# Moving half of one branch's softmax scaling to VectorE, and reordering scores, transposes and scaling

## The reference, cut to what matters

```python
s = einsum('bqhgd,bkhd->bhgqk', q, k) * scale      # + mask, + sink in swa
p = softmax(s)
o = einsum('bhgqk,bkhd->bqhgd', p, v)
x = x + gate * (sum over branches of sigmoid(g) * ((o * silu(z)) @ w_o)) @ w_out
```

## Time and profile before

| | us |
|---|---|
| median of 3 runs (1754.3 to 1757.47) | 1756.91 |
| the profiled execution | 1756.88 |
| its span in the profile | 1755.1 |

### The profile page before, as it was taken

The page is one execution under the profiler, slowest core; times in us unless marked ns, Lnnn a source line. Parts: engine busy times, 40 slices in busy tenths (PEclk is TensorE's granted clock), DMA queues, the critical chain, the costliest instruction groups (busy, mean ns, idle before and its releaser), DMA issues.

```text
span 1755.1 us, 26992 instructions
## 1 busy us (share of the span) xinstructions
PE 1679.7 (96%) x10400; PEld 1471.6 (84%) x10400; DVE 1037.7 (59%) x2164; ACT 1049.0 (60%) x1919; POOL 625.0 (36%) x426
## 2 busy tenths in 40 slices
PE   7899999999999999999999999999999998999997
PEld 3778888889888899999889996788888887888787
DVE  6445766665566655545774556566676666555633
ACT  3435777776667767765221254678777678777322
POOL 2433333333333332323322344344344433333442
PEclk9999999999999999999999999999999999999999
DMA  9111111111121112012635222111122221212642
GB/s 332 40 37 29 26 46 37 49 31 49 49 55 49 42 31 55 26 48 57 219 117 197 90 87 61 41 38 46 51 53 67 72 73 32 69 52 53 204 148 93
DMA packets 178531, 129.51 MB, mean 74 GB/s; under 512 B 21658, under 2 KB 167652, under 8 KB 178404
## 3 DMA queue, kind: packets, MB, share of 16 engines
q1 hardware_dynamic: 174240, 115.36, 23.0%
q10 hardware_dynamic: 2884, 8.24, 1.3%
q0 software_dynamic: 1280, 4.20, 0.7%
HBM read 123.58 MB, written 4.19 MB: 73 GB/s over the span
## 4 chain that ended last, share of the span: by engine, by line
PE 77%; DVE 11%; ACT 8%; issue 3%; DMA 1%; POOL 1%; SPq 0%; DVEq 0%; ACTq 0%
PE acc L1393 56%; PE wide L1444 6%; PE ptp L1462 6%; PE pv L1475 4%; PE pv L1476 3%; DVE nmax L2051 2%; ACT e L1710 2%; DVE pt L2076 1%; ACT w_hi L1627 1%; DVE k_m L1579 1%; DVE q_s L1579 1%; ACT k_m L1570 1%; DVE k_s L1579 1%; DMA w_raw<-in_ada_w 1%; ACT e L1717 0%
## 5 line engine op out<-in xcount | busy, mean ns | idle before, releaser
L1834 POOL TENSOR_TENSOR w_lo<-w_raw,w_hi 128x1024 fp32r<-128x1024 f32 (+2 forms) x192 | 390.9, 2039 | 566.4 <-ACT w_hi L1627 565.0
L1393 PE MATMUL acc<-h_hi,w_hi 128*128 128x512 f32 (+2 forms) x1320 | 466.1, 354 | 13.0 <-DVE lf L1954 5.1
L1393 PE MATMUL acc<-h_hi,w_lo 128*128 128x512 f32 (+2 forms) x1320 | 462.4, 351 | 0.0
L1393 PE MATMUL acc<-h_lo,w_hi 128*128 128x512 f32 (+2 forms) x1320 | 458.6, 351 | 0.5 <-POOL h_lo L1896 0.5
L1393 PEld LDWEIGHTS acc<-h_hi,w_hi 128*128 128x128 f32 (+1 forms) x1320 | 249.5, 189 | 52.0 <-issue 12.4
L1725 ACT ACTIVATE pt<-ptp 128x512 fp32r<-128x512 f32 (+3 forms) x312 | 165.9, 563 | 198.2 <-PE ptp L1462 196.4
L1393 PEld LDWEIGHTS acc<-h_hi,w_lo 128*128 128x128 f32 (+1 forms) x1320 | 249.8, 189 | 34.0
L1393 PEld LDWEIGHTS acc<-h_lo,w_hi 128*128 128x128 f32 (+1 forms) x1320 | 246.9, 189 | 34.8 <-POOL h_lo L1896 0.9
L2051 DVE TENSOR_REDUCE nmax<-wide 128x1 f32<-128x768 f32 (+3 forms) x240 | 190.0, 792 | 112.1 <-PE wide L1444 108.6
L1888 POOL TENSOR_TENSOR o_t<-o_half,o_t 64x256 f32<-64x256 f32 x120 | 91.9, 766 | 436.9 <-DVE o_half L2083 434.8
L1717 ACT ACTIVATE e<-e,einv 128x768 f32<-128x768 f32 (+3 forms) x240 | 193.4, 806 | 57.2 <-DVE einv L2068 56.8
(11 more groups left out here) (215 smaller groups left out, 3065.8 us busy)
## 6 DMA issues: line engine op xcount, KB each, us to landing
w_raw<-in_w_in SPq DMA_DIRECT2D x102, 512.0 KB, 3.9
w_raw<-in_ada_w SPq DMA_DIRECT2D x48, 512.0 KB, 5.3
w_raw<-in_w_out SPq DMA_DIRECT2D x16, 512.0 KB, 3.5
w_raw<-in_w_in SPq DMA_DIRECT2D x16, 256.0 KB, 3.2
w_raw<-in_w_o_mla SPq DMA_DIRECT2D x16, 256.0 KB, 2.7
w_raw<-in_w_o_swa SPq DMA_DIRECT2D x16, 256.0 KB, 2.7
w_raw<-in_w_o_ax SPq DMA_DIRECT2D x16, 256.0 KB, 2.8
w_raw<-in_mla_w_uq SPq DMA_DIRECT2D x16, 144.0 KB, 2.3
```

The source lines that it names most:

```text
L1393: ins = nc.tensor.matmul(dst, lhs, rhs, start=first, stop=last)
L1834: nc.gpsimd.tensor_tensor(w_lo[s][:, 0:k], w_raw[s][:, 0:k], f(w_hi[s][:, 0:k]), ALU.subtract).then_inc(w_lo_ready, 1)
```

## The change

Three things change. The order of events: the transposes T come behind the score part SB instead of ahead of it, and behind N and OC too, so that on ScalarE the scaling and the output copy stand ahead of the rounding copies. The engine: units of the first branch (`mla`) with an odd number are scaled by VectorE, 40 of the 80 units of that branch. The place: VectorE's scaling is a new event NS, behind X, while its reciprocal stays in N.

```diff
             valued, waiting = waiting[:2], waiting[2:]
-            for t in valued:
-                T(t)
             if u:
                 SB(u)
             if 0 < i <= len(units):
                 emit("N", u=units[i - 1])
+            if turned:
+                emit("OC", pa=turned)
+            for t in valued:
+                T(t)
             if u:
                 X(u)
-            if turned:
-                emit("OC", pa=turned)
+            if 0 < i <= len(units):
+                emit("NS", u=units[i - 1])
             for t in valued:
                 emit("TL", t=t)
...
-        on_act, invs, norms = BRANCHES, {}, {}
+        invs, norms = {}, {}
+
+        def on_act(u):
+            return u["branch"] != BRANCHES[0] or u["n"] % 2 == 0
+
...
                 elif ev == "T":
                     t = e["t"]
-                    u = t["pa"]["units"][-1]
-                    if u["branch"] in on_act:
-                        if new(norm_act, invs[u["n"]]):
-                            pe.wait_ge(norm_act, invs[u["n"]])
-                    elif new(norm_done, norms[u["n"]]):
-                        pe.wait_ge(norm_done, norms[u["n"]])
+                    for u in t["pa"]["units"]:
+                        if on_act(u):
+                            if new(norm_act, invs[u["n"]]):
+                                pe.wait_ge(norm_act, invs[u["n"]])
+                        elif new(norm_done, norms[u["n"]]):
+                            pe.wait_ge(norm_done, norms[u["n"]])
...
-                    if u["branch"] in on_act:
+                    if on_act(u):
                         nc.vector.reciprocal(einv[:, r:r + 1], total[:, r:r + 1]).then_inc(inv_done, 1)
                         continue
                     link(nc.vector.reciprocal(einv[:, r:r + 1], total[:, r:r + 1]))
+                elif ev == "NS" and not on_act(e["u"]):
+                    u = e["u"]
+                    r = u["n"] % 8
                     nc.vector.tensor_scalar(e_of(u), e_of(u), einv[:, r:r + 1], None, ALU.mult).then_inc(norm_done, 1)
```

More of the change, by code:

```diff
@@ L1198, in _ @@
                     sp.wait_ge(out_saved[i], 16 * (TT - TT_CTX) // 2)
-        on_act, invs, norms = BRANCHES, {}, {}
+        invs, norms = {}, {}
+        def on_act(u):
+            return u["branch"] != BRANCHES[0] or u["n"] % 2 == 0
         for e_ in events:
             if e_["ev"] == "N":
-                counts = invs if e_["u"]["branch"] in on_act else norms
+                counts = invs if on_act(e_["u"]) else norms
                 counts[e_["u"]["n"]] = len(counts) + 1
@@ L1711, in _ @@
                                          bias=nbias[:, r:r + 1], scale=scale, accum_out=esum[:, r:r + 1]).then_inc(exp_done, 1)
-                elif ev == "N" and e["u"]["branch"] in on_act:
+                elif ev == "N" and on_act(e["u"]):
                     u = e["u"]
```

## The result

The changed kernel takes 1795.59 us (median of 4 runs, 1791.58 to 1803.38) against 1755.95 us before: a ratio of 1.023, with a 95% interval of 1.0215 to 1.0245. It is slower, as forecast, but by 40 us and not by 5; the time lies 20 us above the stated range.

The account below looks back on a forecast made before the run. TensorE was taken as the bound, idling mainly in waits for VectorE. The terms 12 + 5 + 4 - 2 - 4 = +15 us, some 10 given back, left +5 us on 1756.88: 1762 us, range 1744 to 1775.

Parts of the forecast that it names:

- step 1: ScalarE's scaling and output copy ahead of the rounding copies: VectorE's subtraction, then TensorE, resume some 0.75 us later, +12 us.
- What bounds the kernel: TensorE holds 77% of the chain that ended last; the change can only move TensorE's idle time.
- Both releasers: What ends the values product's waits: VectorE's subtraction (16 times, 20.6 us) and VectorE's output sum (15 times, 10.6 us).
- The lower end: Rounding moved back on ScalarE: where VectorE is not late, scaling fills ScalarE's wait for transposes; 0 or a gain.
- Step 2: VectorE scales 40 units of the first branch, 22.4 us more work there, partly exposed to TensorE: +5 us.
- GpSimd's hold: VectorE's new scalings blocked by GpSimd instructions on SBUF: 17 us more on VectorE, a small part exposed.
- Step 3: Scores ahead of transposes: TensorE idles for the exponential, +4 us; the maximum starts earlier, -2 us.
- Step 4: ScalarE's relief: the exponential no longer stands behind a scaling in even iterations; half of 8 us reaches TensorE, -4 us.
- given back: Some 10 us of the +15 us sum taken off: waits give VectorE time to catch up, and terms share iterations.

Follow-up runs that it names:

- e12: Kernel before with ScalarE's scaling and output copy ahead of its rounding copies, and the scaling cut to 2 columns of each unit: 1764.25 us, ratio 1.0046.
- e3: Kernel before with only ScalarE's order changed, scaling and output copy ahead of the rounding copies; ScalarE scales all units: 1800.24 us, ratio 1.0246.
- e13: Full change with one thing put back, ScalarE's rounding copies ahead of scaling and output copy; VectorE keeps its 40 scalings: 1774.91 us, 1.0107 against the kernel before.
- e2: Kernel before, order of events kept, with VectorE scaling the 40 odd units of the first branch behind the maximum: 1771.39 us, ratio 1.0087.
- e4: Kernel before with only TensorE's order changed, scores ahead of transposes; ScalarE scales all units in its old order: 1765.58 us, ratio 1.0048.
- e1: Kernel before with the whole changed order of events, but ScalarE scaling all 240 units as before: 1794.89 us, ratio 1.0212.
- e5: Kernel before, order of events kept, with VectorE scaling the 40 odd units of the first branch behind the subtractions: 1765.64 us, ratio 1.0049.
- e11: Kernel before, in its own order, with ScalarE's scaling cut to 2 columns of each unit: 1753.14 us, ratio 0.9978.
- e9: Kernel before with VectorE's subtractions ahead of the maximum: 1795.57 us, ratio 1.0230.
- e10: Kernel before with VectorE's subtractions and the output sum both ahead of the maximum: 1860.78 us, ratio 1.0593.

## Why the prediction went wrong

The direction and the ranking of the steps were right. The time was not, for three reasons: step 1 was counted in far too few iterations, 10 us were taken off for which nothing stood, and the clock was left out. The first weighs most: with nothing taken off the sum was 15 us, still 25 us short.

- **What bounds the kernel.** Half right. Both releasers are VectorE before and after. But "can only move the idle time of TensorE" failed: 20.7 us of the 40.2 were idle time, the other 19.5 us were busy time for the same matmuls.
- **Step 1, +12 us: the failing term.** Right in mechanism (0.75 us worked out, 0.79 by the times written there, 0.74 in the trace; e12 shows that the durations in a row decide). Mis-sized: I priced only the waits that existed. Alone it costs 43 us (e3), within the change 21 us (e13 to the full change). 15 new waits of TensorE came, and VectorE waits 109 times for the rounding where it was 29: iterations without a wait before were hit too. How much slack each of them had, I did not measure. The lower end (0 or a gain, the scaling filling time in which ScalarE waited for the transposes) did not come: that wait fell from 196.4 to 88.6 us, and TensorE's idle time rose all the same.
- **Step 2, +5 us.** Alone 14.5 us (e2), with scores ahead of transposes 9.3 us (e4 to e13), on top of the whole order about 1 us. That step 1's delay covers it fits these numbers: only with the rounding behind does it vanish. GpSimd's hold was 6 us on VectorE, not 17.
- **Step 3, +4 - 2 us.** Alone 8.7 us (e4): 7 us more of score waits, and 1.9 us by the account of the clock. In the full change its sign fell short: 3.5 us of score waits against 1.1 before, not 4 to 8 us of new ones. On top of step 1 it turns into a gain of 5 us, which I had not seen. My reading is that earlier scores help just the iterations in which ScalarE is late; the maximum's waits for scores, 122.2 us in e3 and 88.6 in e1, fit it.
- **Step 4, -4 us.** Not seen as a gain in any run; e5, with the relief and the scaling out of the way, is still 9 us slower. ScalarE was 34 us less busy, as forecast (1049.0 to 1015.1). e11 cuts all of ScalarE's scalings from 193 to 70.1 us and gains 4 us. In the order of before, ScalarE's load counts for little.
- **The sum: given back, -10 us.** The whole sum stood at +15 us; I then took 10 us off as "given back". No row stood for it, and no run shows it: the idle time alone rose by 20.7 us. Given back would mean that a wait makes later waits shorter; that these waits begin with a projection's results and are made anew by them is my reading of timelines like the one of unit 19, not a measurement.
- **The clock, left out.** I priced a wait at its own length. The granted clock stood at 0.99 in the stretches, and I did not ask what followed the one wait of 2.1 us there. By the account it is 15 us of the 40. The accounts of the parts, worked out in the same way from span, busy time and mean clock: e3 is 41.9 us longer in span, 21.6 us idle and 16.7 us clock; e1 33.2, 21.2 and 5.8; e2 13.8, 8.1 and 5.5; e4 9.3, 6.8 and 1.9. The rest of each, 0.2 to 6 us, stays unexplained (e1's trace is of its fastest run; the clocks of its other three, 0.976 to 0.980, would make 13 to 20 us in place of 5.8); the first matmul behind a wait is seen longer (0.36 us against 0.28), which may be part of it.

Two things on record bear the account out. Busy time less the time lost to the clock is 1656 to 1663 us in the traces of the kernel before, the full change and all experiments but e9 and e10, while busy time itself goes from 1679 to 1700 us; in e9 and e10 it is 1667 and 1680 us, so there something else adds to busy time. And the four executions of the changed kernel, the same program each time, have spans of 1789.6, 1791.9, 1795.3 and 1801.4 us at clocks of 0.983, 0.980, 0.979 and 0.976: 11.8 us for 0.007, where the account says 12.6.

Open: no run takes the clock's falls away and leaves the waits, so its share is an account and not an experiment, and what decides whether a wait is followed by a fall is not shown. The parts don't add up (43 + 9 + 14 us alone, 40 together). e1, e4 and e13 show where it is lost: on top of step 1, step 3 is worth -5 us in place of 9, and step 2 then 1 us in place of 14. Why is a reading only.

## What to carry to other kernels

In engines that work through queues in order, an instruction that needs a late result must not stand ahead of one that doesn't, even if it fills idle time on average: add up, on both sides of the next meeting point, what must run in a row after the late result. A delay put on a meeting point is to be counted in every iteration whose slack is smaller than it, not only where a wait is seen already. And a wait of TensorE can have a second price, the lower clock behind it: look at the granted clock in the windows behind the longest waits before pricing more of them.

## What the runs showed of the hardware

A wait of TensorE of 1.9 us was followed by a window of 4 us at a granted clock of 0.57, while the wait of 1.18 us at the same place before was followed by 1.00. Of the nine waits of 1.9 us and more in the attention after, seven came with such a fall. VectorE's scaling of 128x768 in SBUF took 0.61 us in the median and up to 1.49 us when GpSimd worked on SBUF operands; the 0.615 us interpolated from 512 and 1024 columns held.
